# Four in-place products on VectorE, the difference and the sum on GpSimd: u's spectrum in a two-block kernel

## What is computed

```python
def bidir_long_conv(u, k):
    L = u.shape[1]
    uf = jnp.fft.rfft(u.astype(jnp.float32), n=2 * L, axis=1)
    kf = jnp.fft.rfft(k, n=2 * L, axis=0)
    y = jnp.fft.irfft(uf * kf[None], n=2 * L, axis=1)[:, :L]
    return y.astype(u.dtype)

def hyena_branch(z_hy, conv_w, conv_b, filt, hy_bias):
    z = short_conv(z_hy, conv_w, conv_b)
    x0, x1, v = jnp.split(z, 3, axis=-1)
    k = hyena_kernel(z.shape[1], *filt)
    u = v * x1
    y = bidir_long_conv(u, k) + u * hy_bias
    return y * x0
```

## Time and profile before

| what | value |
|---|---|
| median of 3 runs | 1321.17 us |
| lowest, highest | 1321.11, 1323.73 us |
| the profiled execution | 1319.96 us |
| its span in the profile | 1318.2 us |
| TensorE busy | 1262.8 us (96%) |
| VectorE busy | 845.6 us (64%) |
| ScalarE busy | 583.7 us (44%) |
| GpSimd busy | 53.5 us (4%) |

### The profile page before, as it was taken

How to read it: one execution, slowest core, us unless ns; L and a number is a source line. 1 busy time by engine, 2 the same in 40 slices (tenths; PEclk the granted TensorE clock), 3 DMA queues, 4 the chain that set the end, 5 groups by cost and what they waited for, 6 DMA issues and landing times.

```text
span 1318.2 us, 19274 instructions
## 1 busy us (share of the span) xinstructions
PE 1262.8 (96%) x7713; PEld 1106.3 (84%) x7713; DVE 845.6 (64%) x1334; ACT 583.7 (44%) x929; POOL 53.5 (4%) x67
## 2 busy tenths in 40 slices
PE   6999999999899999999999999999899998999997
PEld 6887999977788888887886998788588996999986
DVE  5875788786687777744424674267766666655544
ACT  6654545444622222222326652246244744544443
POOL 2030002000000000001000000010000000000000
PEclk9999999999999999999999999999999999999999
DMA  8444577775376678853241443233123544455562
GB/s 321 145 135 142 194 241 248 229 236 188 101 229 198 193 243 294 286 185 112 83 141 57 160 144 98 94 112 128 65 81 95 180 158 145 161 187 180 181 194 89
DMA packets 59465, 219.29 MB, mean 166 GB/s; under 512 B 6684, under 2 KB 6720, under 8 KB 58608
## 3 DMA queue, kind: packets, MB, share of 16 engines
q1 hardware_dynamic: 56736, 205.55, 47.5%
q0 software_dynamic: 2352, 11.76, 2.6%
q10 hardware_dynamic: 288, 0.75, 0.2%
HBM read 216.95 MB, written 1.07 MB: 165 GB/s over the span
## 4 chain that ended last, share of the span: by engine, by line
PE 81%; DVE 9%; ACT 6%; issue 3%; DMA 1%; POOL 0%; DVEq 0%; SPq 0%; ACTq 0%
PE ps L1979 18%; PE ps L1981 17%; PE ps L1980 17%; ACT hi L628 3%; PE ps L2025 3%; PE ps L2026 3%; PE ps L2027 3%; PE ps L2036 3%; PE ps L2038 3%; PE ps L2037 3%; DVE lo L1204 2%; PE ps L2015 1%; PE ps L2017 1%; PE ps L2016 1%; PE ps L2527 1%
## 5 line engine op out<-in xcount | busy, mean ns | idle before, releaser
L1204 DVE TENSOR_TENSOR lo<-raw,hi 128x1024 fp32r<-128x1024 f32 x316 | 388.7, 1232 | 322.8 <-ACT hi L628 322.4
L1979 PE MATMUL ps<-nh,hi 128*128 128x256 f32 (+1 forms) x1784 | 555.8, 312 | 19.2 <-DVE lo L1204 13.0
L1980 PE MATMUL ps<-nh,lo 128*128 128x256 f32 (+1 forms) x1784 | 548.3, 307 | 0.0
L1981 PE MATMUL ps<-nl,hi 128*128 128x256 f32 (+1 forms) x1784 | 548.1, 307 | 0.0
L628 ACT ACTIVATE hi<-raw 128x1024 fp32r<-128x1024 f32 x316 | 333.0, 1056 | 436.4 <-PE ps L1981 245.3
L1979 PEld LDWEIGHTS ps<-nh,hi 128*128 128x128 f32 x1784 | 342.3, 192 | 49.4 <-DVE lo L1204 16.9
L1980 PEld LDWEIGHTS ps<-nh,lo 128*128 128x128 f32 x1784 | 342.7, 192 | 16.2 <-issue 0.7
L1981 PEld LDWEIGHTS ps<-nl,hi 128*128 128x128 f32 x1784 | 342.5, 192 | 15.2
L642 ACT ACTIVATE sg<-ps 128x256 f32<-128x256 f32 (+1 forms) x66 | 30.0, 455 | 132.5 <-PE ps L1981 132.5
L1191 DVE SCALAR_TENSOR_TENSOR raw<-raw,cvec 128x1024 f32<-128x1024 f32 x72 | 86.8, 1222 | 1.4
L2025 PE MATMUL ps<-hi,H 128*128 128x512 f32 x176 | 70.0, 398 | 3.9 <-DVE lo L1204 3.7
(11 more groups left out here) (346 smaller groups left out, 1283.0 us busy)
## 6 DMA issues: line engine op xcount, KB each, us to landing
raw<-in_up SPq DMA_DIRECT2D x132, 512.0 KB, 4.0
raw<-in_in SPq DMA_DIRECT2D x86, 512.0 KB, 3.7
raw<-in_w_ada SPq DMA_DIRECT2D x72, 512.0 KB, 4.7
raw<-in_down SPq DMA_DIRECT2D x66, 512.0 KB, 4.3
raw<-in_out SPq DMA_DIRECT2D x8, 512.0 KB, 3.8
raw<-in_hy_out SPq DMA_DIRECT2D x8, 512.0 KB, 3.7
raw<-in_da_out SPq DMA_DIRECT2D x8, 512.0 KB, 3.7
raw<-in_o SPq DMA_DIRECT2D x8, 512.0 KB, 3.6
```

Of the source, the lines that this page charges most:

```text
L1204: dve.tensor_tensor(lo[:, h, 0:w], raw[:, r, 0:w], hi[:, h, 0:w].bitcast(F32), ALU.subtract).then_inc(lo_done, 1)
L1979: mm(o, hi[:, h, wk], x_hi, start=first, stop=False)
L1980: mm(o, lo[:, h, wk], x_hi, start=False, stop=False)
L1981: return mm(o, hi[:, h, wk], x_lo, start=False, stop=last)
```

## The change

VectorE makes only the four products of a quarter. The first two go to `yt` as before; the third and fourth are written over `kim` and `kre`. GpSimd makes the difference of the first two (into `proj`) and the sum of the last two (into `spec_im`). TensorE's next transform waits for the fourth product (`im_products`) and no more for the sum. The first two products of the next quarter, and `convolved`, wait for the difference (`re_summed`). The inverse transforms wait for four sums and four differences.

```diff
@@ GpSimd, behind the loop over hy_v @@
+            for g in range(4):
+                ft, half = g // 2, g % 2
+                w = slice(half * 512, half * 512 + 512)
+                kr, ki = (k[:, ft, w].rearrange("p (a n) -> p a n", a=2) for k in (kre, kim))
+                pool.wait_ge(sem("re_products"), g + 1)
+                pool.tensor_tensor(halves(proj, ft, half), yt[:, 0:2, :], yt[:, 2:4, :], ALU.subtract)\
+                    .then_inc(sem("re_summed"), 1)
+                pool.wait_ge(sem("im_products"), g + 1)
+                pool.tensor_tensor(halves(spec_im, ft, half), ki, kr, ALU.add).then_inc(sem("yf_ready"), 1)
@@ VectorE, spectrum(g) @@
                 dve.wait_ge(sem("uf_ready"), g + 1)
                 if g:
-                    dve.wait_ge(sem("yf_ready"), g)
+                    dve.wait_ge(sem("re_summed"), g)
                 step(dve.tensor_tensor(t0, kr, ur, ALU.mult))
-                after(step(dve.tensor_tensor(t1, ki, ui, ALU.mult)))
-                after(step(dve.tensor_tensor(halves(proj, ft, half), t0, t1, ALU.subtract)))
-                step(dve.tensor_tensor(t0, ki, ur, ALU.mult))
-                after(step(dve.tensor_tensor(t1, kr, ui, ALU.mult)))
-                dve.tensor_tensor(halves(spec_im, ft, half), t0, t1, ALU.add).then_inc(sem("yf_ready"), 1)
+                dve.tensor_tensor(t1, ki, ui, ALU.mult).then_inc(sem("re_products"), 1)
+                after(n)
+                dve.wait_ge(sem("re_products"), g + 1)
+                step(dve.tensor_tensor(ki, ki, ur, ALU.mult))
+                dve.tensor_tensor(kr, kr, ui, ALU.mult).then_inc(sem("im_products"), 1)
@@ VectorE, before convolved @@
-                            dve.wait_ge(sem("yf_ready"), 4)
+                            dve.wait_ge(sem("re_summed"), 4)
@@ TensorE, spectrum(g) and inverse(j) @@
                 if g:
-                    pe.wait_ge(sem("yf_ready"), g)
+                    pe.wait_ge(sem("im_products"), g)
...
                 pe.wait_ge(sem("yf_ready"), 4)
+                pe.wait_ge(sem("re_summed"), 4)
```

## The result

The changed kernel's median is 1313.2 us (1311.62 to 1315.81, 6 runs) against 1321.96 before (1321.08 to 1323.73, 6 runs): ratio 0.9934, 95% interval 0.9923 to 0.9945. In a second session it was 1315.23 (5 runs) against 1321.26 (20 runs), ratio 0.9955 (0.9940 to 0.9969). The kernel is faster, as forecast, but by 8.8 and 6.0 us, not 5.3: 1313.2 lies under the range's lower end, 1314.4.

What follows compares the result with a forecast made beforehand. TensorE, 81% of the chain, was taken as the bound; its stalls from 923 to 961 us, 6.84 less 0.32 and 1.25, gave 5.27. Span 1318.2 less 5.3 is 1312.9, on the runs' median 1315.9 us; range 1314.4 to 1319.0.

Steps and rivals of the forecast that it cites:

- 6.84 less 0.32 and 1.25 is 5.27 us: TensorE's four stalls, 923 to 961 us: 6.84 in all, 0.32 staying before transform 2, 1.25 before slab 17.
- 6.8 us is the most that the change can give here: Upper limit on the gain: all TensorE stall before transforms 1 to 3 and slab 17 removed.
- the shift should last to the end: Behind the stage nothing is tied to a clock time, so the whole span shortens by 5.3 us.
- transform 1: TensorE's transform after VectorE's quarter 0: starts 1.08 us earlier, its whole stall gone, slack 0.38.
- transform 2: TensorE's transform after quarter 1: VectorE allows it 2.54 us earlier, a stall of 0.32 stays.
- transform 3: TensorE's transform after quarter 2: starts 3.81 us earlier, when TensorE is ready, slack 0.19.
- slab 17: TensorE's slab products after quarter 3 and slab 15's taps: 5.27 us earlier, 1.25 us of stall stay.
- the slower rival: Products three and four wait for GpSimd's subtraction, the taps for its addition: 1323.7 us, or 1325.2; chance 0.07.
- 1318.6: Rival: GpSimd holds back the fourth product alone, quarter 3.42 us, 2.6 us won in four legs; chance 0.07.
- 1321.2: Rival: GpSimd holds back the taps as well, or the gain is lost behind the stage; chance 0.10.
- The mix that was expected to lose up to 0.2: VectorE's map mix (L1780) before transform 3 would meet the last 0.1 to 0.2 us of GpSimd's addition.
- The late sum: Rival: the first inverse waits for GpSimd's last addition; needs over 3.2 us of delay; no chance of its own.

Runs made afterwards that it cites:

- one_wait: Changed kernel with slab 15's taps ahead of quarter 3 and without VectorE's wait for product one before product three: 1314.81 us.
- vector_all: Changed kernel without GpSimd: VectorE makes the four products first, then the difference and sum itself; TensorE waits for the fourth product: 1317.99 us, ratio 0.9971.
- old_taps_first: Kernel before, with slab 15's taps moved ahead of quarter 3 at p = 16 and nothing else changed: 1317.62 us, ratio 0.9969.
- slab_late: Changed kernel with four needless VectorE operations ahead of slab 15's taps at p = 16, lengthening slab 17's wait: 1318.62 us.
- late_sum: Changed kernel with GpSimd's sum of quarter 3 made four times in place of once: 1317.39 us.

## Why the prediction was wrong

**The step that failed** is the sum "6.84 less 0.32 and 1.25 is 5.27 us", taken as all that the change gives. The range's lower end stands on it too ("6.8 us is the most that the change can give here"), and so does the step to the whole ("each engine there waits for another engine's instruction, so the shift should last to the end"). The 5.27 came out, and the shift does last. But the sum has no term for TensorE's clock: it was put at nothing, without a reason, and it isn't nothing. In some executions a wait of TensorE costs 1.5 us behind it besides its length, and a half-clock stretch 130 us further on can come or go with an edit of this stage. The sum that the runs show, before to changed:
- stage, waits: 5.3
- stage, clock: 1.5 in two of four profiles, so about 0.7
- tail, clock near 1090: 1.6, in every profile

Together 7.6, against 7.5 between the medians of all listed runs. The 8.8 of the first comparison holds another 1.2 us or so. Its likely place is the head, which the change doesn't touch: it took 921.9 to 924.5 us in both kernels, 923.5 on average in before and 923.7 in the changed kernel, and the stretch from 35 to 40 us is in one of four profiles of before and in three of five of the changed kernel. It says nothing on the change.

The Trainium skill has this, in TensorE: Matmul & The Clock Gate, Part 1: TensorE has two clock states and idling sends it back to the lower. The traces agree: 1.00 before the 2.55 us wait and 0.76 in the window behind it, in two of the four profiles of before. The prediction should have had a term for this: the stretches near 35 and 1093 us were there to be read in the trace of before (0.67; 0.80 and 0.86), and their price came out as 1.46 and 1.6 us. But that trace has none behind the stage's own waits, and that the one near 1093 would go could not be read from it.

**The steps that held.** Distances from transform 0 (from the earlier trace rows, with its start at 923.34, and from the rows above):

| us earlier | forecast | measured |
|---|---|---|
| transform 1 | 1.08 | 1.09 |
| transform 2 | 2.54 | 2.54 |
| transform 3 | 3.81 | 3.83 |
| slab 17 | 5.27 | 5.28 |

That close is in part luck. In the legs to transform 2 and to slab 17 the quarter's extra 0.07 us is offset: VectorE's search for the largest scores starts 4.71 and 4.70 us behind the transform before it, where it was 4.78 in the kernel before, and nobody had forecast that. In the other two legs the slack swallows the 0.07.

- The quarter: 2.60 forecast, 2.67 measured. The 0.07 is the second wait before product three, shown by one_wait. Writing in place cost nothing.
- GpSimd: 1.26 to 1.30 per operation (1.30 forecast). It started 0.08 behind product two, not 0.14. With the second wait before product three this put GpSimd's difference 0.02 ahead of product three (926.88, 926.90), which the slower rival needs; the product wasn't held even so.
- VectorE's wait at p = 18, called a wait for four sums, is one for four differences (`re_summed`). Nothing in the forecast hangs on it.
- Collisions: products and taps were not held. The rivals on that (1318.6, 1321.2, 1323.7) fall with the 0.69 and 0.68 over GpSimd's 926.88 to 928.18 and the tap's 0.48 inside the sum of 937.42. The Trainium skill's rule (SBUF — State Buffer, Who interferes with whom) holds in both directions here: one SBUF input, no delay; two, a mix of 1.50 for 0.75 and a split of 2.32 for 1.22. The mix that was expected to lose up to 0.2 lost nothing, but it met the sum for 0.02 us, not for the 0.1 to 0.2 forecast.
- The late sum: 3.1 us of cover measured, 3.2 forecast. The Trainium skill's rule that elementwise work belongs on VectorE (GPSIMD Engine Reference, Engine selection) did not decide: vector_all, which follows it, is 2.8 us slower in its session and 3.8 slower than the median of all changed runs.
- The eight added waits on `inverse` cost nothing that shows: the tail is 352.4 us in the changed kernel and in old_taps_first, which doesn't have them.

**What stays open**: why the stretch near 1090 comes in one kernel and not in another, so that 1.6 of the 7.6 us is counted and not explained; and how often the clock falls behind slab 17 in before, where two of four is a small count.

## What to carry to other kernels

Follow a handoff leg by leg, taking at each leg the later of the two engines: four legs came out within 0.02 us. Then give a removed TensorE wait its length plus a chance of one half-clock stretch behind it, and compare kernels at equal granted clock, or part by part, before believing a total. A gain of 1 us in one stage can be paid back 130 us later, behind a wait that nobody touched.

## What had not been expected of the hardware

- A stretch at 1.2 GHz behind a TensorE wait of 2.2 to 3.6 us: in slab_late, late_sum and vector_all, and in two of four profiles of before; not in the other two, and in no stage whose longest wait was 1.6 us or less (11 profiles). Near 1090, behind a wait of 2.1 us that every kernel has, the stretch is in all profiles of some kernels and in none of others.
- It costs 1.5 us where slab products stand (4.43 for 2.93), 1.6 in the tail.
- Two waits in a row on VectorE, both on its own operations, take 0.07 us more than one.
- GpSimd and VectorE lengthen each other's work where both have two SBUF inputs: 1.79 us for a sum of 1.27, 2.32 for a split of 1.22, 1.50 for a mix of 0.75. One mix inside such sums kept its 0.75.
